# Splitting the 512-column matmuls of seven blocks into two of 256 within one PSUM bank

## The reference

```
h = rms_norm(x, norm_g)
u, v, z = jnp.split(h @ w_in, 3, axis=-1)      # w_in: 2048 x (3 * 4096)
u = jax.nn.gelu(u)
v = rms_norm(jax.nn.gelu(v), v_norm_g)
mixed = einsum(w_causal, v) + b_s              # 16 groups of 256 channels
y = u * mixed * jax.nn.silu(z)
x = x + y @ w_out
```

## Time and profile before

| | us |
|---|---|
| median of 3 runs | 2532.03 |
| lowest, highest | 2531.23, 2532.59 |
| span of the profiled execution (the trace shows no other time of it) | 2531.9 |
| TensorE busy in that span | 2471.0 |
| VectorE busy | 1140.0 |
| ScalarE busy | 797.2 |

### The profile page before, as it was taken

One profiled execution on the slowest core, in us unless ns is written; L12 is line 12 of the kernel. 1 busy time (PEld: TensorE's weight loads), 2 busy tenths in 40 slices (PEclk: granted clock), 3 DMA queues, 4 the chain that ended last, 5 costly groups with the idle time before them and its releaser, 6 DMA issues.

```text
span 2531.9 us, 32556 instructions
## 1 busy us (share of the span) xinstructions
PE 2471.0 (98%) x11310; PEld 2033.2 (80%) x11310; DVE 1140.0 (45%) x1762; ACT 797.2 (31%) x1594; POOL 76.1 (3%) x116
## 2 busy tenths in 40 slices
PE   9999999999999999999999999999979999999689
PEld 7888888888888888888888878888758888888567
DVE  3222224555555545544455744544334444454236
ACT  5333332222222222222222353333223333333233
POOL 0000000000000000000000000000000000000000
PEclk9999999999999999999999999999989999999899
DMA  5333333333323333333333335445575446445853
GB/s 166 101 96 96 99 94 98 94 104 99 97 94 102 94 100 96 95 95 95 104 98 96 93 78 81 95 84 92 55 73 88 93 83 94 85 90 74 47 84 125
DMA packets 260100, 235.93 MB, mean 93 GB/s; under 512 B 14688, under 2 KB 213376, under 8 KB 260048
## 3 DMA queue, kind: packets, MB, share of 16 engines
q1 hardware_dynamic: 256736, 226.55, 40.1%
q0 software_dynamic: 3248, 8.69, 1.6%
q10 hardware_dynamic: 64, 0.02, 0.0%
HBM read 230.97 MB, written 4.23 MB: 93 GB/s over the span
## 4 chain that ended last, share of the span: by engine, by line
PE 63%; issue 36%; POOL 0%; DVE 0%; ACT 0%; DMA 0%; POOLq 0%; SPq 0%; ACTq 0%; DVEq 0%
PE ps L664 10%; PE ps L666 10%; PE ps L665 10%; PE ps L678 9%; PE ps L679 9%; PE ps L680 9%; PE ps L731 1%; PE ps L688 1%; PE ps L934 1%; PE ps L936 1%; PE ps L935 1%; POOL v_all L417 0%; PE ps L847 0%; PE ps L866 0%; POOL qkr L355 0%
## 5 line engine op out<-in xcount | busy, mean ns | idle before, releaser
L452 ACT ACTIVATE w_hi<-w_raw 128x512 fp32r<-128x512 f32 x832 | 516.8, 630 | 1280.6 <-PE ps L666 557.0
L961 DVE TENSOR_TENSOR w_lo<-w_raw,w_hi 128x512 fp32r<-128x512 f32 x832 | 560.7, 689 | 743.0 <-ACT w_hi L452 742.7
L664 PE MATMUL ps<-w_hi,xh 128*128 128x512 f32 x1568 | 630.5, 402 | 41.0 <-DVE w_lo L961 40.1
L666 PE MATMUL ps<-w_hi,xl 128*128 128x512 f32 x1568 | 618.6, 395 | 0.0
L665 PE MATMUL ps<-w_lo,xh 128*128 128x512 f32 x1568 | 617.6, 394 | 0.0
L678 PE MATMUL ps<-xh,w_hi 128*128 128x512 f32 x1024 | 401.3, 392 | 0.0
L680 PE MATMUL ps<-xh,w_lo 128*128 128x512 f32 x1024 | 398.6, 389 | 0.0
L679 PE MATMUL ps<-xl,w_hi 128*128 128x512 f32 x1024 | 398.5, 389 | 0.0
L664 PEld LDWEIGHTS ps<-w_hi,xh 128*128 128x128 f32 x1568 | 298.7, 191 | 113.0 <-DVE w_lo L961 48.9
L666 PEld LDWEIGHTS ps<-w_hi,xl 128*128 128x128 f32 x1568 | 298.7, 190 | 64.7
L665 PEld LDWEIGHTS ps<-w_lo,xh 128*128 128x128 f32 x1568 | 299.6, 191 | 59.2
(11 more groups left out here) (146 smaller groups left out, 1298.0 us busy)
## 6 DMA issues: line engine op xcount, KB each, us to landing
w_raw<-in_a_w_in_dram SPq DMA_DIRECT2D x384, 256.0 KB, 2.8
w_raw<-in_b_w_in_dram SPq DMA_DIRECT2D x256, 256.0 KB, 7.1
w_raw<-in_a_w_out_dram SPq DMA_DIRECT2D x128, 256.0 KB, 2.5
w_raw<-in_b_w_out_dram SPq DMA_DIRECT2D x64, 256.0 KB, 3.0
v_all<-cum_rows POOLq DMA_DIRECT2D x16, 256.0 KB, 10.1
acc<-in_x_dram SPq DMA_DIRECT2D x3, 1024.0 KB, 8.5
out_dram<-acc SPq DMA_DIRECT2D x3, 1024.0 KB, 4.3
vg_row<-in_a_v_norm_g_dram POOLq DMA_DIRECT2D x16, 128.0 KB, 3.6
```

What stands on the lines that cost most here:

```text
L452: act.activation(w_hi[:, s, :], w_raw[:, s, :], ACT.Copy).then_inc(hi_ready, 1)
L664: pe.matmul(ps[S][:, t, :], a, w_hi[:, s, :], start=start, stop=False)
L666: mm = pe.matmul(ps[S][:, t, :], b, w_hi[:, s, :], start=False, stop=stop)
L961: dve.tensor_tensor(w_lo[:, s, :], w_raw[:, s, :], w_hi[:, s, :].bitcast(F32), ALU.subtract).then_inc(lo_ready, 1)
```

## The change

`v_tile` takes the place of `in_tile` in the loop over v blocks 2 to 7, and `in_tile_halves` takes the place of `in_tile_fm` in block `A0`. Each issues the three matmuls first for columns 0 to 255 of the bank and then for columns 256 to 511. Only the first matmul of a bank carries the start flag. Waits, signals, operands, arithmetic and the order of the contraction within each output element stay. The v blocks 0 and 1, the other u/z blocks, the output projections and layer B are as before.

```
+            def v_tile(n, i, k, S):
+                s = i % R
+                pe.wait_ge(lo_ready, n + (i + 1))
+                for t in range(NT):
+                    a, b = xh[:, k, t * P:(t + 1) * P], xl[:, k, t * P:(t + 1) * P]
+                    for c in (slice(0, FB // 2), slice(FB // 2, FB)):
+                        first = k == 0 and c.start == 0
+                        o = ps[S][:, t, c]
+                        pe.matmul(o, a, w_hi[:, s, c], start=first, stop=False, skip_group_check=True)
+                        pe.matmul(o, a, w_lo[:, s, c], start=False, stop=False, skip_group_check=True)
+                        mm = pe.matmul(o, b, w_hi[:, s, c], start=False, stop=k == KC - 1,
+                                       skip_group_check=True)
+                mm.then_inc(tile_used, 1)
...
+            def in_tile_halves(n, i, k, S):
+                s = i % R
+                pe.wait_ge(lo_ready, n + (i + 1))
+                for f in range(FB // P):
+                    a, b = w_hi[:, s, f * P:(f + 1) * P], w_lo[:, s, f * P:(f + 1) * P]
+                    for c in (slice(0, SEQ // 2), slice(SEQ // 2, SEQ)):
+                        first = k == 0 and c.start == 0
+                        o = ps[S][:, f, c]
+                        pe.matmul(o, a, xh[:, k, c], start=first, stop=False, skip_group_check=True)
+                        pe.matmul(o, a, xl[:, k, c], start=False, stop=False, skip_group_check=True)
+                        mm = pe.matmul(o, b, xh[:, k, c], start=False, stop=k == KC - 1,
+                                       skip_group_check=True)
+                mm.then_inc(tile_used, 1)
...
-                        in_tile(j * (2 * KC), S * KC + k, k, S)
+                        v_tile(j * (2 * KC), S * KC + k, k, S)
...
-                in_tile_fm(A0, k, k, 0)
+                in_tile_halves(A0, k, k, 0)
```

## The result

| | before | after |
|---|---|---|
| median of 3 runs, us | 2532.03 | 2547.36 |
| lowest, highest, us | 2531.23, 2532.59 | 2546.31, 2550.87 |
| span of the profiled execution, us | 2531.9 | 2544.7 |

The changed kernel is slower by 0.6%: ratio 1.0063, 95% interval 1.0049 to 1.0078, or 15.3 us by the medians, which is small but clear of the noise. The profiled execution is the run of 2546.31 us, with a span of 2544.7 us, 12.8 us more than the span before.

What follows compares the result with a forecast made beforehand. TensorE was taken to bound the kernel: 1344 splits at 13.3 ns give +17.9 us, 15.3 in the v blocks and 2.6 in `A0`, taking the span from 2531.9 to 2549.8 us; forecast 2550 us, 8-in-10 range 2526 to 2566.

Steps and rivals of the forecast that it cites:

- What bounds the kernel: TensorE, busy 2471.0 of 2531.9 us; in the changed stretch any loss or gain passes straight to the kernel's end.
- The term of the sum: Six v blocks and A0: 1344 splits, each two 120.0 ns halves against 226.7 ns, +17.9 us.
- the step on the floor: In the split blocks, stationary-operand loads keep any half from going below about 110 to 112 ns.
- rival (1): Split blocks: surcharge belongs to the columns, a half takes 113.3 ns, no cost, 2530 to 2535 us; chance 0.27.
- rival (2): Split blocks: halves lack the surcharge and the load bounds them, 111.7 ns each, -4.5 us, 2527.6 us; chance 0.10.
- rival (3): All seven blocks: halves run at the transposes' pace, 109.8 ns, -9.5 us, 2522.5 us; chance 0.06, or better.
- rival (4): Split blocks: load and surcharge add to 125.0 ns, +31.4 us, 2563 us; chance 0.20 shared with an 18 ns surcharge.
- The end time: Whole kernel: span 2549.8 us, plus 0.1 us from span to median, forecast 2550 us.
- everything after 410 us the same, shifted: Stages behind the split blocks, from 410 us on, would stay the same and only start later.
- If the later blocks change their length: A sign, in the blocks after the split ones, that would show the prediction wrong.
- The reason given for the 120.0 ns: Split fp32r matmuls: a fixed preparation of 13.3 ns per instruction on top of 106.7 ns for 256 columns; chance 0.37.
- the 18.0 ns of the forget-gate stream: Forget-gate matmuls, 16-column stationary operands: 231.3 ns each, 18.0 over the columns, read as a cost between instructions.

Runs made afterwards that it cites:

- ladder: The kernel before with chains of 24 extra matmuls of single kinds and lengths ahead of block A0, output thrown away; 2597.40 us.
- v_quarters: Against the kernel before, v blocks 2 to 7 in quarters of 128 columns and A0 in halves; 3061.33 us.
- all_halves: The kernel before with every matmul of tile and in_tile_fm in halves, 9792 of 512 columns in place of 1344; median 2681.03 us, ratio 1.0584.

## Why the prediction was right, and where not

**What bounds the kernel** held. The change lies on TensorE alone, its neighbours took the 15 us as idle time, and every other busy time stayed.

**The term of the sum** held: 1344 splits, 2 x 120.0 ns instead of 226.7, +17.9 us. The windows show +15.37 and +2.49, which is 17.86 us. The load of 111.7 ns stayed hidden, as the step on the floor said. Rivals (1) to (4) fall with their windows of 261, 257, 253 and 288 us against the 276.48 measured.

**The end time** was 2.6 us too high (2550 against 2547.36), and the span 5.1 us (2549.8 against 2544.7), because the forecast had "everything after 410 us the same, shifted". That step failed for the span. Up to 1797 us it holds: the delay stays at 17.3 us. Behind that the two stretches of late weight tiles do not shift as a block, and the profile after has 4.5 us less of delay at its end. "If the later blocks change their length" was one of the prediction's own signs of being wrong, and it came. The rows of the kernel before had shown where: one of its half-clock stretches lies at 1818 us, and TensorE is idle there. The two misses differ because the 0.1 us between span and median failed too: the changed kernel's profiled run took 1.6 us more than its span, and the median lies 1.1 us above that run. The span before had come from an execution slower than the runs of the table, which is why the two spans lie closer than the medians. The 2.6 us by which the median missed are inside the interval of the ratio, so they are not shown to be more than noise.

**The reason given for the 120.0 ns** did not hold as a rule. I called the 13.3 ns a fixed preparation per matmul. With 128 stationary columns it is 13.3 at 512, 496, 384, 320 and 256 columns, but 16.8 at 480, 20 at 448, 10.3 at 264 and at most 11.7 at 240; with narrow operands it is 6.8 to 18.4. That the two lengths of this kernel are among those with 13.3 was luck: no row of the kernel before could tell that 256 columns have the surcharge of 512 while 264 and 448 have not. I had read the 18.0 ns of the forget-gate stream as support for a cost between instructions; the ladder shows that the same 16-column operand at 256 columns costs only 6.8, so that reading was wrong. What rival (1) said, that part of it grows with the columns, fits the ladder at least as well; its 113.3 ns is even what 256 columns take with a 16-column operand. Its price of zero for the split was wrong because beside a full load of 128 columns they take 120.0 ns. Why the pace settles where it does stays open. Had the kernel's stationary operands been 64 columns wide, 2 x 114.3 - 229.6 = -1.0 ns a split would have been the sum by these chains, and about no change the result (an estimate; no such kernel was run). The prediction also said that the surcharge vanishes in plain fp32; the last two chains of `ladder` leave 2.5 ns, 429.2 and 215.8 ns for each of the two records of a call at 512 and 256 columns.

## What to carry to other kernels

Where TensorE is saturated, cost a change of matmul length as count x (new pace - old pace), with paces taken between starts and not from durations, and take the loads of the stationary operand as a second bound, since each piece carries its own. A surcharge found at one length is a measurement at that length: one kernel with chains of the lengths in question settles it in a single run. Keep pieces long enough to cover their load, because below that each piece costs the load's pace, and in the one run whose pieces were all that short the granted clock fell after a gap of 1.8 us and did not come back for 655 us, though TensorE worked on almost without a pause.

## What the runs showed of the hardware

- Fp32r matmuls at 2.4 GHz settle at 226.7 ns for 512 columns and 120.0 for 256 with 128 stationary columns; bf16 ones at 216.1 and 109.1; plain fp32 ones take two records a call, 429.2 ns each at 512 columns and 215.8 at 256 (`ladder`), which is two cycles a column and 2.5 ns.
- Paces of fp32r chains are not smooth in the columns: 448 take 206.5 ns, 464 take 209.7; 256 and 264 both take 120.
- In `v_quarters`, with quarters of 128 columns each 111.7 ns, the granted clock fell to 1.2 GHz after 175 us, 1.6 us after a gap of 1.81 us on TensorE, and stayed there for 655 us of work with a single gap of 0.4 us. It rose 2.3 us after the last quarter.
- In `all_halves`, with loop bodies of twice the length, gaps of 2.2 to 2.6 us stand at six jumps of the layer A loop and of up to 14.3 us in layer B. It moved 177 instruction packets in place of 31, 52 of them between 600 and 1300 us, where the kernel before moved none.
